# A two-part fp32 transformer kernel: filler of the first block in another order, and the convolutions of the state space model as steps of their own

## The reference

```
# first block, layer l:  x -> twelve projections h = x @ w_in
ya = softmax(q_a k_a' - alibi) v_a  * silu(a_z)            # 8 heads ("moba"; one block of 256 tokens)
q_b = rope(rmsnorm(b_cq) @ w_uq);  k_b, v_b = rmsnorm(b_ckv) @ w_ukv, rope(b_kr)
yb = softmax(q_b k_b') v_b  * silu(b_z)                    # 8 heads ("mla")
yc = rmsnorm((softmax1 - lam * softmax2) v_c) * silu(c_z)  # 4 heads ("diff")
g = sigmoid(x @ w_m + b_m)                                 # gates a, b, c, each 1024 wide
merged = ga * (ya @ w_a) + gb * (yb @ w_b) + gc * (yc @ w_c)
r = ALPHA * x + merged @ w_o
r = r + sigmoid(r @ w_pg) * (p @ w_p);  x = layernorm(r)
# second block, layer l: feed-forward, mixers, feed-forward; of the mixers:
proj = u @ w_in_2          # r_q r_k r_v r_g | s_q s_k s_v | m_z | m_x m_bc | m_dt
xbc = silu(causal_conv1d(m_x, m_bc; 4 taps) + conv_b)      # 1024 channels
dt = softplus(m_dt + dt_bias)                              # steps of the state space model
# retention (r), stick-breaking attention (s), state space scan (m), then @ w_out_2
# modulations: shift, scale and gate vectors, c @ ada_w, for the whole second block
```

## Time and profile before

| | |
|---|---|
| median of 3 runs | 1953.12 us |
| the profiled execution's own time | 1959.57 us |
| its span | 1958.3 us |
| PE busy | 1856.0 us, 95% |
| DVE busy | 1326.9 us, 68% |
| ACT busy | 957.8 us, 49% |
| chain that ended last | PE 65%, DVE 21%, ACT 11%, DMA 2% |
| DMA | 389.69 MB, mean 199 GB/s |

### The profile page before, as it was taken

The page is one execution under the profiler, slowest core; times in us unless marked ns, Lnnn a source line. Parts: engine busy times, 40 slices in busy tenths (PEclk is TensorE's granted clock), DMA queues, the critical chain, the costliest instruction groups (busy, mean ns, idle before and its releaser), DMA issues.

```text
span 1958.3 us, 34201 instructions
## 1 busy us (share of the span) xinstructions
PE 1856.0 (95%) x15080; PEld 1788.6 (91%) x15080; DVE 1326.9 (68%) x1799; ACT 957.8 (49%) x1320; POOL 60.4 (3%) x76
## 2 busy tenths in 40 slices
PE   7998988999989989899989999999999999999998
PEld 7987888989879889899989899999999989899998
DVE  5666667765676766776676767667766676857664
ACT  5564464455645544644446335444544456335443
POOL 0000100000001000100000001000000000000000
PEclk9998899989989999899989999999999899999999
DMA  7453546564344456466535434666466556244562
GB/s 308 174 195 125 199 156 237 186 236 173 143 167 189 179 214 237 160 243 258 238 137 229 173 132 170 249 258 246 173 252 258 200 195 237 112 169 168 233 258 94
DMA packets 59283, 389.69 MB, mean 199 GB/s; under 512 B 6656, under 2 KB 9472, under 8 KB 15232
## 3 DMA queue, kind: packets, MB, share of 16 engines
q1 hardware_dynamic: 59136, 387.52, 51.6%
HBM read 386.45 MB, written 1.05 MB: 198 GB/s over the span
## 4 chain that ended last, share of the span: by engine, by line
PE 65%; DVE 21%; ACT 11%; DMA 2%; issue 1%; SPq 0%; DVEq 0%; ACTq 0%
PE banks L772 16%; PE banks L773 16%; PE banks L774 16%; DVE weights_split L920 8%; ACT weights_split L914 5%; PE bank L773 4%; PE bank L774 4%; PE bank L772 4%; DMA weights<-in_weights 2%; ACT map L1355 2%; DVE weights L900 1%; DVE xbc L2369 1%; DVE map_stat L1543 1%; ACT map L1361 1%; PE bank L840 1%
## 5 line engine op out<-in xcount | busy, mean ns | idle before, releaser
L920 DVE TENSOR_TENSOR weights_split<-weights,weights_split 128x2048 fp32r<-128x2048 f32 (+2 forms) x306 | 656.9, 2148 | 356.7 <-ACT weights_split L914 355.8
L914 ACT CAST weights_split<-weights 128x2048 fp32r<-128x2048 f32 (+2 forms) x306 | 542.9, 1776 | 105.6 <-PE bank L774 70.4
L772 PE MATMUL banks<-u,weights_split 128*128 128x256 f32 (+1 forms) x1648 | 465.1, 282 | 12.1 <-DVE weights_split L920 8.7
L773 PE MATMUL banks<-u,weights_split 128*128 128x256 f32 (+1 forms) x1648 | 460.7, 280 | 0.0
L774 PE MATMUL banks<-u,weights_split 128*128 128x256 f32 (+1 forms) x1648 | 460.4, 279 | 0.0
L772 PEld LDWEIGHTS banks<-u,weights_split 128*128 128x128 f32 (+1 forms) x1648 | 311.8, 189 | 15.7 <-DVE weights_split L920 9.8
L772 PE MATMUL banks<-x,weights_split 128*128 128x256 f32 x1056 | 301.7, 286 | 15.7 <-DVE weights_split L920 11.4
L773 PEld LDWEIGHTS banks<-u,weights_split 128*128 128x128 f32 (+1 forms) x1648 | 312.1, 189 | 0.4
L774 PEld LDWEIGHTS banks<-u,weights_split 128*128 128x128 f32 (+1 forms) x1648 | 312.0, 189 | 0.4
L774 PE MATMUL banks<-x,weights_split 128*128 128x256 f32 x1056 | 295.9, 280 | 0.0
L773 PE MATMUL banks<-x,weights_split 128*128 128x256 f32 x1056 | 295.9, 280 | 0.0
(11 more groups left out here) (331 smaller groups left out, 3058.1 us busy)
## 6 DMA issues: line engine op xcount, KB each, us to landing
weights<-in_weights SPq DMA_DIRECT2D x262, 1024.0 KB, 6.9
weights<-in_ada SPq DMA_DIRECT2D x80, 1024.0 KB, 4.8
weights<-in_weights SPq DMA_DIRECT2D x36, 512.0 KB, 5.5
weights<-in_weights SPq DMA_DIRECT2D x4, 576.0 KB, 5.6
constants_second<-in_constants_second SPq DMA_DIRECT2D x1, 1792.0 KB, 8.6
weights<-in_weights SPq DMA_DIRECT2D x2, 640.0 KB, 7.4
h<-in_x SPq DMA_DIRECT2D x2, 512.0 KB, 5.3
out<-xbc SPq DMA_DIRECT2D x4, 256.0 KB, 2.2
```

Source lines behind the costliest of these rows:

```text
L772: pe.matmul(out, left[0], right[0], start=start, stop=False, **more)
L773: pe.matmul(out, left[0], right[1], start=False, stop=False, **more)
L914: act.do.copy(split[:, 0, 0:n], raw[:, 0:n]).then_inc(*self.act_wrote.inc(("weights", key)))
L920: dve.do.tensor_tensor(split[:, 1, 0:n], raw[:, 0:n], split[:, 0, 0:n].bitcast(F32), ALU.subtract).then_inc(*self.dve_wrote.inc(("weights" ...
```

## The change

Six moves, all in the list of steps; the panels in memory follow the same new order (`plan`).

1. `merge` yields gates 0, 1, branches 0, 1, gates 2, 3, branches 2, 3 instead of gate and branch in turn, and the first branch of each two comes in the same step as the second (`run`).
2. In the filler the gates and branches of a come before the queries of mla.
3. Of gate_b only panels 0 and 1 are in the filler; panel 2 comes after the heads, then branch 0, gate 3, branches 1 to 3.
4. The first half of `ple` (with the split of p) is the filler's last item, the second half takes its old place ahead of w_out. p is loaded two heads earlier.
5. A convolution is a step of its own: 0 and 1 come behind the second panel of m_x, 2 and 3 behind the first of m_bc, 4 behind the second, 5, 6 and 7 behind the panels of s_q and the first of s_k.
6. Two `unit_done` calls fall in the part where modulations are paused, so each modulation of the first block stands one half to two halves later in the list.

```diff
@@ plan
-        for pair in zip(gates, products):
-            yield from pair
+        gates, products = list(gates), list(products)
+        for j in (0, 2):
+            yield from gates[j:j + 2] + products[j:j + 2]
...
@@ first_layer
         def merge(branch, after):
-            while after not in self.done:
-                yield
-            for j in range(DC // MERGE_BLOCKS):
-                yield from self.dense("gate_" + branch, l, [j])
-                yield from self.dense("branch_" + branch, l, [j])
+            for j in (0, 2):
+                yield from self.dense("gate_" + branch, l, [j, j + 1])
+                while after not in self.done:
+                    yield
+                self.run(self.dense("branch_" + branch, l, [j]))
+                yield from self.dense("branch_" + branch, l, [j + 1])
...
+            yield from merge("a", ("ya", l))
             yield from mla_q()
-            yield from merge("a", ("ya", l))
             yield from mla_kv()
             yield "MLA can start"
             yield from self.dense("b_z", l, range(2))
             yield from merge("c", ("ycn", l))
-            yield from self.dense("gate_b", l, range(DC // MERGE_BLOCKS))
+            yield from self.dense("gate_b", l, [0, 1])
+            self.add("split_p", l)
+            self.run(self.dense("ple", l, [0], 2))
+            yield
...
         self.pause_mods()
-        for i, _ in enumerate(self.dense("branch_b", l, range(DC // MERGE_BLOCKS))):
-            if i == 1:
-                self.add("split_p", l)
+        self.run(self.dense("gate_b", l, [2]))
+        self.run(self.dense("branch_b", l, [0]))
+        self.run(self.dense("gate_b", l, [3]))
+        self.run(self.dense("branch_b", l, [1, 2, 3]))
         for at in (4, 6):
             self.add("split_merged", l, at)
-        self.run(self.dense("ple", l, [0], 2))
+        self.run(self.dense("ple", l, [1], 2))
         self.mods_pause = False
         self.run(self.dense("w_out", l, range(4)))
-        self.run(self.dense("ple", l, [1], 2))
         self.run(self.dense("ple_gate", l, range(4)))
@@ mixers
-        self.run(self.dense("m_x", l, range(2)))
-        self.run(self.dense("m_bc", l, range(2)))
+        def with_convolutions(product, chunks):
+            for _ in product:
+                for c in chunks.pop(0):
+                    self.add("convolution", l, c)
+                yield
+        self.run(with_convolutions(self.dense("m_x", l, range(2)), [(), (0, 1)]))
+        self.run(with_convolutions(self.dense("m_bc", l, range(2)), [(2, 3), (4,)]))
         self.run(self.dense("m_dt", l, [0]))
 
         def fill():
-            yield from self.dense("s_q", l, range(2))
-            yield from self.dense("s_k", l, range(2))
+            yield from with_convolutions(self.dense("s_q", l, range(2)), [(5,), (6,)])
+            yield from with_convolutions(self.dense("s_k", l, range(2)), [(7,), ()])
```

More of the change, by code:

```diff
@@ L121, in plan @@
         yield from w_in("w_in", IN1, l, ["a_q", "a_k", "a_v", "a_z", "c_q", "c_k", "c_v", "c_z"])
+        yield from merge(l, 0, "a")
         yield from panels("uq", l, "mla_w_uq", Q_LORA, 0, 768, 384)
-        yield from merge(l, 0, "a")
         yield from panels("ukv", l, "mla_w_ukv", KV_LORA, 0, 1024, 1024)
@@ L126, in plan @@
         yield from merge(l, 2, "c")
-        yield from panels("gate_b", l, "w_merge", D, D, D, MERGE_BLOCKS * P)
-        yield from panels("branch_b", l, "w_branch_b", W, 0, D, MERGE_BLOCKS * P)
+        gates = list(panels("gate_b", l, "w_merge", D, D, D, MERGE_BLOCKS * P))
+        products = list(panels("branch_b", l, "w_branch_b", W, 0, D, MERGE_BLOCKS * P))
         ple = list(panels("ple", l, "w_ple", PLE, 0, D, D // 2))
-        yield ple[0]
+        yield from gates[0:2] + ple[0:1] + gates[2:3] + products[0:1] + gates[3:4] + products[1:4] + ple[1:2]
         yield from panels("w_out", l, "w_out", D, 0, D, 256)
-        yield ple[1]
         yield from panels("ple_gate", l, "w_ple_gate", D, 0, D, 256)
@@ L348, in head @@
                 filler.until("MLA can start")
-                if h == HEADS - 1:
+                if h == HEADS - 3:
                     self.loads.append(("p", l))
@@ L2014, in scalar_second @@
                 self.scalar_modulated(*at)
+            elif what == "convolution":
+                l, c = at
+                act.wait_ge(self.dve_wrote, ("conv", l, c))
+                act.do.activation(b["xbc"][:, c, :], b["xbc"][:, c, :], ACT.Silu,
+                                  bias=self.s(f"conv_b{l}", 1, c)).then_inc(*self.act_wrote.inc(("xbc", l, c)))
             elif what == "steps":
@@ L2102, in scalar_second_bank @@
             self.products.emptied(bank_name, self.act_wrote, bank_name)
-            for c in (at, at + 1):
-                act.wait_ge(self.dve_wrote, ("conv", l, c))
-                act.do.activation(t["xbc"][:, c, :], t["xbc"][:, c, :], ACT.Silu,
-                                  bias=self.s(f"conv_b{l}", 1, c)).then_inc(*self.act_wrote.inc(("xbc", l, c)))
     def shifts(self, l, at):
@@ L2266, in vector_second @@
                 dve.do.memset(b["xbc_in"][:, :, 0:TAPS - 1], 0.0).then_inc(*self.dve_wrote.inc(("pad", l)))
+            elif what == "convolution":
+                self.vector_convolution(*at)
             elif what == "steps":
@@ L2358, in vector_second_bank, with vector_convolution @@
             self.vector_silu(key, t[name])
-        elif name in ("m_x", "m_bc"):
-            at = 2 * u + 4 * (name == "m_bc")
-            dve.wait_ge(self.act_wrote, bank_name)
-            for c in (at, at + 1):
-                src, dst = t["xbc_in"], t["xbc"]
-                tap = lambda i: self.s(f"conv_w{l}", 1, 8 * i + c)
-                dve.do.tensor_scalar(dst[:, c, :], src[:, c, 0:T], tap(0), None, ALU.mult).then_inc(
-                    *self.dve_wrote.inc())
-                for i in range(1, TAPS):
-                    dve.wait_ge(self.dve_wrote, LAST)
-                    dve.do.scalar_tensor_tensor(dst[:, c, :], src[:, c, i:i + T], tap(i), dst[:, c, :], ALU.mult,
-                                                ALU.add).then_inc(
-                        *self.dve_wrote.inc(*[("conv", l, c)] * (i == TAPS - 1)))
+    def vector_convolution(self, l, c):
+        dve, src, dst = self.dve, self.b["xbc_in"], self.b["xbc"]
+        tap = lambda i: self.s(f"conv_w{l}", 1, 8 * i + c)
+        dve.wait_ge(self.act_wrote, ("bank", (("m_x", "m_bc")[c // 4], l, c // 2 % 2), 0))
+        dve.do.tensor_scalar(dst[:, c, :], src[:, c, 0:T], tap(0), None, ALU.mult).then_inc(*self.dve_wrote.inc())
+        for i in range(1, TAPS):
+            dve.wait_ge(self.dve_wrote, LAST)
+            dve.do.scalar_tensor_tensor(dst[:, c, :], src[:, c, i:i + T], tap(i), dst[:, c, :], ALU.mult,
+                                        ALU.add).then_inc(*self.dve_wrote.inc(*[("conv", l, c)] * (i == TAPS - 1)))
     def vector_add_to_h(self, tag, c):
```

## The result

The changed kernel takes 1936.05 us, median of 4 executions (1930.44 to 1938.59), beside 1953.32 us (4 executions, 1953.06 to 1958.24) of the kernel before on the same chip: ratio 0.9903, 95% interval 0.9884 to 0.9922. So it is faster, by about 17 us; forecast were 1932 us, and a range of 1912 to 1950. Its profiled execution is the fastest of the four, 1930.44 us (span 1929.0 us), 29.1 less than that of before.

The account below looks back on a forecast made before the run. PE, 95% busy, bounds the kernel, so only its waits and slow clock give time. Gains 15.6 + 7.6 + 6.4, losses 7.2 and 1.0: 21.4 us off the profiled 1959.57, then 6.45 to the median: 1932, range 1912 to 1950.

Parts of the forecast that it names:

- Term A: From mla's first query bank to b_z: fewer waits and less slow clock, gain 16.3 us in layer 0, 9.3 in layer 1.
- Term B: b_z to the first gate of c: a wait and slow clock go, gain 2.9 and 2.4 us.
- D: After the mla heads: gates b 2 and 3 between branches cover the products, gain 1.2 and 1.3 us.
- E: Before ple_gate: the second half of ple leaves, with the wait of 1.15 us; gain 0.9 us a layer.
- Term C: Among the mla heads: gate c 2, gate b 0 and ple 0 wait 11.2 us; loss 5.7 and 6.3.
- Term F: Mixers: s_q waits go, smaller ones come at s_k 1, s_v 0, s_v 1; net gain 3.2 us each.
- Term G: Slow clock behind new waits: loss of 3.6 us a layer (7.2) among the heads, 1.0 in the mixers.
- What costs nothing: A modulation moved to the last feed-forward, the earlier p load, POOL's copies and convolutions as steps add no time.
- The first: Rival: waits among the mla heads don't come, Term C and Term G at nothing or better; 1912 us, chance 0.14.
- The second: Rival: first-block waits only move, rotations still wait 2.13 to 4.75 us; 1949 us, chance 0.15 for 1943 to 1950.
- The third: Rival: PE stays at the 1.2 GHz level from gate c 2 to ple 0 in each layer; 1969 us, chance 0.10.
- The fourth: Rival: the low part of s_q 0 stays late and the mixers give nothing; 1938 us, chance 0.10.

Follow-up runs that it names:

- the other two traces with the old order: Traces of two runs on the kernel before: only the convolutions as steps (0.9968), and only pairs of c with the new tail (1.0025).
- late rotations: Kernel before with only the four rotations of the queries moved behind the branches of a, ahead of the keys of mla: 1956.81 us, ratio 1.0010.
- two banks: Kernel before with two banks of the mla queries in a filler step, 36 matmuls between turns instead of 18: 1946.41 us, ratio 0.9957.
- the new order alone: Kernel before with only the new order of the first block, mixers as before: 1941.69 us, ratio 0.9932.
- c and tail alone: Kernel before with pairs of c, gates b 2 and 3 among the branches of b, and ple 0 in the filler: 1961.21 us, ratio 1.0025.
- c in turn: Changed kernel with gates and branches of c in turn again: 1938.67 us, ratio 0.9925 to the kernel before.
- early p: Changed kernel with the cast and low part of p one filler item earlier, between gates b 0 and 1: 1928.73 us, ratio 0.9871 to the kernel before.
- later convolutions: The early p kernel with convolutions 5, 6 and 7 one item later in the mixers: 1920.41 us, ratio 0.9831 to the kernel before.

## Why the prediction was right, and where not

**Term A** had its mechanism right and its size too large. 15.7 for 16.3 in layer 0 looks like a hit and is luck: against the other two traces with the old order the new one gains 10.2 to 12.0 us there and 5.0 to 5.6 in layer 1, for 16.3 and 9.3. I had counted as gain all that the one trace of before showed, with the wait of 2.76 in `ukv`, for which the move of the branches gave no reason. In layer 1 it came out at 5.7: the last queries' rotation and the keys', right behind others with no matmuls between them, waited 0.59 and 1.00 where I had put 0.7 for all of it, and the slow clock behind them cost 1.5. That the branch of a carries the gain is shown by the run with it alone. Both halves of my reason are seen at work: the rotations gone from between the softmaxes of diff give some 4 and 3 us where they stood (late rotations; the run as a whole, 1.0010, gives this back at the new place), and more matmuls as cover give about 3 a layer (two banks, 0.9957). How the rest of the 15 to 18 us divides, with 48 matmuls for 36 and the branches in pairs, no run separates.

**Term B** came as forecast (2.7 and 2.5 for 2.9 and 2.4), and so did **D** and **E** within 0.6 us each.

**Term C** is the step that was mis-sized. The waits are where I put them, but 2.21, 0.88 and 3.32 in layer 0 and 2.18, 1.29 and 3.10 in layer 1, 6.4 and 6.6 us together for 11.2: a loss of 1.0 and 1.7 us for 5.7 and 6.3. The chain behind the softmax that I had added up, ACT's cast, DVE's low part and the branch's product, stands in the trace link by link ahead of gate c 2 at 248.12:

```profile
243.17 1.89 ACT L923 CAST weights_split<-weights 128x2048 fp32r<-128x2048 f32 x1
...
245.09 2.29 DVE L929 TENSOR_TENSOR weights_split<-weights,weights_split 128x2048 fp32r<-128x2048 f32 x1 [2.66 <-ACT weights_split L923]
247.30 0.68 DVE L1500 SCALAR_TENSOR_TENSOR gate<-gate,banks 128x512 f32<-128x512 f32 x1
```

What I had too small is PE's work beside it: the two branches and the head's small matmuls take 7.9 us (237.99 to 245.91), not some 7. And the softmax does not stand at the same place each time: its last step on DVE comes 4.3 us behind the first of the two branches ahead of gate c 2, but 2.7 ahead of gate b 0, which waits 0.88 where I had 2.9. For ple 0 the chain through p was right, and moving p took the wait away.

**Term F** held, to the engine and to 0.3 us: s_q 0 free, 2.15 at s_k 1 for 2.2, 0.77 at s_v 0 for 0.95, 3.5 a mixer for 3.2. (The 3.2 left out my own 0.35 at s_v 1; no such wait came.) By my estimate from the drain of 1380 ns that the Trainium skill gives ("ScalarE: Activation LUTs", section "What ACT_TABLE_LOAD costs") only 0.4 a mixer was to be left. After the loads at 997.43 and 999.20 the next instruction starts 1.29 us later each time, so this trace again shows no drain.

**Term G** was 8.2 us; 3.0 came in the profiled execution, and in layer 0 only, 1.5 behind gate c 2 (48 matmuls in 7.26 us) and 1.5 behind ple 0.

**What costs nothing** was not quite nothing. Before the second block's first panel PE waits 6.54 us in every kernel with the new tail (the changed one and five of the experiments: the new order alone, c and tail alone, c in turn, early p, later convolutions) and 5.33 in those with the old one. There is one modulation more behind the first block; I didn't follow the chain there, so that this is the cause is argued, not shown.

**The conversion.** I took the profiled execution as 6.45 us above the median, as before. In the changed kernel it lies 5.6 below it. The 6.45 could not carry over: Some 4 to 5.5 us of it stood in the very stretch that term A rewrites, and I took them off twice, once as A's gain and once here. So that the forecast, 21 us below the trace and 1932 in all, came within 4 us of the 1936 measured is partly luck, two errors of opposite sign: C and G 15 us too dark, this one 12 too bright. Of the signs that I named, the rotations, s_q 0, s_k 1 and s_v 0 came; the 8 to 9 us in layer 1, and waits of 3 us at gate c 2 and gate b 0, did not.

**Rivals.** The first (no waits among the heads) was nearest in size for terms C and G, a loss of 5.7 us for its nothing and my 20, but the waits exist. The second (waits only move) fell in the first block. The third, slower by the clock, shows its head in the run with pairs of c and the tail alone: 1.0025 at the lowest clock of all. What it lacks is the half clock held from wait to wait: the windows are back at 1.00 before the next wait. The fourth fell, s_q 0 was free.

## What to carry to other kernels

In a ring of matmul, vector work and matmul again, count both the matmuls that stand between the two and the foreign work on the vector engine; here each was worth some 3 to 4 us a layer. When you take work out of such a place, give it one with matmuls around it, or it costs there what it gave. A small late operand (here p) is moved one item earlier; a chain that only stands in the way (here the softplus) moves the wait along with it, and what helped was to take away the work in front of it. Judge parts one at a time: here one of three parts of the first block made all the gain. And before you book a wait as gain, look for it in a second trace of the same order.

## What the runs showed of the hardware

The granted clock differs between executions of one program, and the time goes with it. Of 54 executions of the kernel before, those at a mean clock of 0.965 took 1958.0 us on average, those at 0.970 1953.3, those at 0.974 1949.7: about 1 us for each 0.001. One profiled execution is then uncertain by some 5 us either way, more than most of the terms here; the medians of several executions show the size, and one trace only the place.

After waits of the same length the clock may or may not fall (2.21 us: 0.66 in the window behind; 2.18 us: 1.00). So a price for a wait's slow clock is a chance times 1.5 to 2 us, not a fixed sum.
